# Two rounds of 32 tokens for expert pairs of 33 to 64, and a router that chooses tile by tile, in a float32 kernel of four layers

## What is computed

```
g_prob = softmax(t @ rg_w + rg_b)                     # 4 groups
g_p, g_idx = top_k(g_prob, 1)
e_logits = (t @ re_w + re_b).reshape(n_tok, 4, 8)[chosen group]
e_p, e_idx = top_k(softmax(e_logits), 2)              # 2 of the group's 8 experts
gate = g_p * e_p / sum(e_p);   expert = g_idx * 8 + e_idx
# each expert e, on the tokens that chose it:
hg, hu = split(x @ w_gu[e], 2)                        # 1024 -> 512 and 512
y = (silu(hg) * hu) @ w_down[e]                       # 512 -> 1024
out = sum over a token's two experts of gate * y
```

## Time and profile before

| | us |
|---|---|
| median of 3 runs | 2333.54 |
| lowest, highest | 2332.27, 2340.67 |
| the profiled execution | 2336.21 |
| its span, first to last instruction | 2334.4 |

### The profile page before, as it was taken

One profiled execution on the slowest core, in us unless ns is written; L12 is line 12 of the kernel. 1 busy time (PEld: TensorE's weight loads), 2 busy tenths in 40 slices (PEclk: granted clock), 3 DMA queues, 4 the chain that ended last, 5 costly groups with the idle time before them and its releaser, 6 DMA issues.

```text
span 2334.4 us, 30929 instructions
## 1 busy us (share of the span) xinstructions
PE 1858.1 (80%) x13622; PEld 1234.3 (53%) x13622; DVE 594.2 (25%) x964; ACT 388.7 (17%) x738; POOL 17.0 (1%) x18
## 2 busy tenths in 40 slices
PE   7999999999999875766666887599986575876664
PEld 5788875788876644222224563475983233622211
DVE  1223222224221343121111101455345221111112
ACT  2233102233111221100000000142221000000001
POOL 0000000000000000000000000001000000000000
PEclk9999999999999966888878998799997798989887
DMA  8312343422344306999999674213013799699996
GB/s 320 104 73 102 146 162 133 114 77 106 133 177 185 122 0 244 427 424 426 424 426 421 242 289 185 73 45 136 5 60 136 326 424 425 240 387 424 425 425 251
DMA packets 51160, 539.59 MB, mean 231 GB/s; under 512 B 7393, under 2 KB 16097, under 8 KB 17665
## 3 DMA queue, kind: packets, MB, share of 16 engines
q1 hardware_dynamic: 49248, 527.13, 55.8%
q0 software_dynamic: 864, 6.29, 0.7%
q10 hardware_dynamic: 832, 2.98, 0.3%
HBM read 535.33 MB, written 1.05 MB: 230 GB/s over the span
## 4 chain that ended last, share of the span: by engine, by line
PE 68%; DMA 16%; DVE 6%; issue 6%; ACT 4%; DVEq 0%; ACTq 0%
PE ps L399 50%; PE ps L406 16%; DMA arena<-in_moe_w_down 4%; DMA arena<-in_moe_w_gu 4%; DMA ring<-in_moe_w_gu 4%; DMA ring<-in_moe_w_down 3%; PE ps L412 2%; DVE arena L1254 2%; DVE x L1265 1%; ACT arena L2003 1%; ACT arena L2007 1%; DVE mT L1254 1%; ACT hb L2003 1%; ACT L2003 0%; DVE hb L1254 0%
## 5 line engine op out<-in xcount | busy, mean ns | idle before, releaser
L399 PE MATMUL ps<-hT,ring 128*128 128x256 f32 (+2 forms) x1888 | 389.5, 371 | 0.0
L399 PEld LDWEIGHTS ps<-hT,ring 128*128 128x128 f32 (+2 forms) x1888 | 329.2, 184 | 53.2 <-issue 3.4
L406 PE MATMUL ps<-arena 128*32 128x512 f32 (+2 forms) x1556 | 255.9, 706 | 121.2 <-issue 86.3
L406 PE MATMUL ps<-ring,arena 128*32 128x512 f32 (+1 forms) x1440 | 219.9, 683 | 99.2 <-issue 69.9
L2007 ACT ACTIVATE arena<-ps 128x512 f32<-128x512 f32 (+3 forms) x139 | 90.9, 654 | 905.0 <-PE ps L406 540.0
L1254 DVE TENSOR_TENSOR arena<-arena,ps 128x256 f32<-128x256 f32 (+3 forms) x88 | 51.7, 588 | 704.1 <-ACT arena L2003 610.0
L406 PEld LDWEIGHTS ps<-arena 128*32 128x32 f32 (+2 forms) x1556 | 68.6, 132 | 286.3 <-issue 232.0
L399 PE MATMUL ps<-arena 64*64 64x64 f32 (+10 forms) x1808 | 169.5, 299 | 51.2 <-ACT arena L2266 22.3
L406 PEld LDWEIGHTS ps<-ring,arena 128*32 128x32 f32 (+1 forms) x1440 | 62.2, 126 | 238.4 <-issue 197.3
L399 PEld LDWEIGHTS ps<-arena 64*64 64x64 f32 (+3 forms) x1808 | 114.0, 167 | 107.8 <-ACT arena L2266 50.6
L399 PE MATMUL ps<-ring,hT 128*128 128x256 f32 (+4 forms) x576 | 151.4, 422 | 8.7 <-ACT hT L2003 7.0
(11 more groups left out here) (150 smaller groups left out, 1397.8 us busy)
## 6 DMA issues: line engine op xcount, KB each, us to landing
ring<-in_moe_w_gu SPq DMA_DIRECT2D x64, 2048.0 KB, 26.3
arena<-in_moe_w_gu SPq DMA_DIRECT2D x64, 2048.0 KB, 29.0
arena<-in_moe_w_down SPq DMA_DIRECT2D x32, 2048.0 KB, 31.0
ring<-in_moe_w_down SPq DMA_DIRECT2D x32, 2048.0 KB, 30.4
ring<-in_w_merge SPq DMA_DIRECT2D x16, 2048.0 KB, 7.7
ring<-in_w_in SPq DMA_DIRECT2D x10, 2048.0 KB, 7.4
ring<-in_attn_w_qkv SPq DMA_DIRECT2D x6, 2048.0 KB, 8.0
ring<-in_rw_w_rkv SPq DMA_DIRECT2D x6, 2048.0 KB, 7.3
```

Source lines behind the costliest of these rows:

```text
L399: i = t.matmul(o, l, r, start=first, stop=last, skip_group_check=True)
L406: i = t.matmul(o, l, r, start=first, stop=last, skip_group_check=True)
```

## The change

Four edits:

1. **Middle path.** It now serves pairs of 33 to 64 tokens (`2 * CAP`, CAP is 32), in two rounds on each weight chunk. Round 0 takes the 32 tokens that are already in `xe`; only tokens 32 to 63 are gathered (into `x2`). All its matmuls have the small path's form, once for each round.
2. **Full path.** Its text is the same, but it serves pairs of more than 64 tokens, where it served those of more than 128.
3. **Router.** Each tile's router matmuls stand right behind its transposes in `out_proj`, and VectorE chooses tile by tile, with 16 operations for each. A rising table (1000 - index) lets one scalar_tensor_tensor and a maximum find the first of the greatest.
4. **Behind the first gather.** Both Exp calls, the gate values and the flags come after the one-hot matrix on which the gather waits (`"0 oh"`). The names `"da end"` and `"rw end"` now stand ahead of the layer norms, and the waits of all engines for each other at the start of `moe` are gone.

The core of the diff:

```
-            p = tile(name, (act, name + " out a"), (dve, name + " out b"))
...
+            p = tile(f"moe{l} route{i}", (dve, f"moe{l} logits{i}"))
+            t.wait_ge(*act(name + " out a"))
+            t.wait_ge(*dve(name + " out b"))
+            mm([(p[:, 0:36], hT[:, k, i * P:(i + 1) * P], m.rw36[:, l, k, :], k == 0, k == KT - 1) for k in range(KT)], f"moe{l} route{i}")
...
-        t.wait_ge(*dve(M + "0 places"))
+        t.wait_ge(*dve(M + "0 oh"))
         for half in range(2):
             gather(psum[0][:, 512 * half:512 * half + 512], half, M + f"first gather{half}")
+        t.wait_ge(*dve(M + "0 places"))
         gates_T(psum[1][:, 0:512], M + "first gatesT")
...
-                    lst = [(buf[:, k * P:(k + 1) * P], x[:, i, k * P:(k + 1) * P], oh24[:, i, a, :], i == 0, i == 1)
-                           for a, buf in enumerate((pg, pt)) for k in range(KT) for i in range(NT)]
+                    lst = [(psum[1][:, k * 64:(k + 1) * 64], x[:, i, k * P:(k + 1) * P], e.oh2[:, i * 64:(i + 1) * 64], i == 0, i == 1)
+                           for k in range(KT) for i in range(NT)]
...
-                        mm_to([(bufs[a][:, n * P:(n + 1) * P], gv[q][:, kk, a * D + n * P:a * D + (n + 1) * P], e.xm[a][:, 2 * q + kk, :],
-                                q + kk == 0 and n % 4 == 0, q == 3 and kk == 1) for kk in range(2) for a in range(2) for n in range(8)],
-                              before + 8 + q, N + f"gu{q}")
+                        mm_to([(pg[64 * a + 32 * c:64 * a + 32 * c + 32, 512 * r:512 * r + 512], xs[r][:, 2 * q + kk, a, :],
+                                gv[q][:, kk, a * D + c * 512:a * D + (c + 1) * 512], q + kk == 0, q == 3 and kk == 1)
+                               for kk in range(2) for r in range(2) for a in range(2) for c in range(2)], before + 8 + q, N + f"gu{q}")
+                    t.wait_ge(*act(N + "m gu"))
+                    tr([(psum[0][:, (4 * r + k) * P:(4 * r + k + 1) * P], g[:, k * P:(k + 1) * P], idn)
+                        for r, g in enumerate((e.gu, e.gu2)) for k in range(4)], N + "m guT")
...
+                        mm_to([(psum[1][64 * n + 32 * a:64 * n + 32 * a + 32, 512 * r:512 * r + 512], hs[r][:, 2 * q + kk, a, :],
+                                dv[q][:, kk, a * D + n * 512:a * D + (n + 1) * 512], q + kk == 0, q + kk == 2)
+                               for kk in range(2) for r in range(2) for n in range(2) for a in range(2)], before + 20 + q, N + f"dn{q}")
...
+        def first_of(dst, val, rising, top):
+            stt(eq, val, top, rising, ALU.is_ge, MUL)
+            red(ix, eq, MAX)
+            ts(dst, eq, ix, None, ALU.is_equal, None)
...
+            ts(cnt2, cnt, 2 * CAP + 0.5, None, ALU.is_gt, None)
```

More of the change, by code:

```diff
@@ L167, in take, with last @@
         return self.tiles[i], old
+    def last(self, name):
+        self.of[name] = len(self.tiles) - 1
+        return self.tiles[-1]
     def __call__(self, name):
@@ L815, in part @@
             return go
-        out_proj("da", d.oT, [(i, part(i)) for i in (1, 0)])
+        out_proj("da", 0, d.oT, [(i, part(i)) for i in (1, 0)])
     def moe(l):
         e, M = m.moe, f"moe{l} "
-        p = tile(M + "route", (dve, M + "logits"))
-        mm(proj_tok(hT, m.rw36[:, l], KT, [p[:, i * 512:i * 512 + 36] for i in range(NT)], slice(0, 36)), M + "route")
         sel = e.sel
-        p = tile(M + "count", (dve, M + "count"))
-        t.wait_ge(*dve(M + "gates"))
+        p = ps.last(M + "count")
+        for i in range(NT):
+            t.wait_ge(*dve(M + f"sel{i}"))
         mm([(p[:, 0:32], tab["st1"], sel[:, 0, :], True, True),
@@ L1210, in part @@
             return go
-        out_proj("rw", r.kT, [(i, part(i)) for i in range(NT)])
+        out_proj("rw", 1, r.kT, [(i, part(i)) for i in range(NT)])
     t.wait_ge(m.consts_landed, 32)
@@ L1561, in layer_norm, with out_proj @@
             stt(x[:, i, :], x[:, i, :], ss[i][:, 1:2], m.lnr[:, 1, :], MUL, ADD, name(i))
-    def out_proj(n, rows, parts):
+    def out_proj(n, l, rows, parts):
         for _, part in parts:
             part()
+        dve.name(f"{n} end")
         for i, _ in parts:
@@ L1570, in out_proj @@
             cp(m.hT[:, 4:8, i * P:(i + 1) * P], ps(f"{n} xT{i}")[:, 512:1024].rearrange("p (k s) -> p k s", k=4), f"{n} xT{i} out b")
-        dve.name(f"{n} end")
-        v.wait_ge(*pe(f"{n} end"))
-        v.wait_ge(*act(f"{n} end"))
+        for i, _ in parts:
+            route(l, i)
     def oT_out(n, dst, i):
@@ L1782, in moe @@
                     after_own()
-                    v.tensor_tensor(acc[:, 1, :], acc[:, 1, :], pt, ADD).then_inc(*dve.to(before + 20, N1 + "all in"))
+                    v.tensor_tensor(acc[:, 1, :], acc[:, 1, :], pg, ADD).then_inc(*dve.to(before + 20, N1 + "all in"))
             with v.Else():
@@ L1972, in part @@
             return go
-        out_proj("rw", 4, [(i, part(i)) for i in range(NT)])
+        out_proj("rw", 1, 4, [(i, part(i)) for i in range(NT)])
     v.wait_ge(m.consts_landed, 32)
@@ L2181, in out_proj @@
             part()
+        act.name(f"{n} end")
         for i, _ in parts:
@@ L2245, in moe @@
         psum = ps.tiles
-        act.name(M + "start")
         g4 = e.ex[:, :, 0:4]
-        s.wait_ge(*dve(M + "group in"))
-        fn(g4, g4, ACT.Exp, M + "group exp")
-        s.wait_ge(*dve(M + "second in"))
-        fn(e.m2, e.m2, ACT.Exp, M + "second exp")
-        act.name(M + "routed")
-        s.wait_ge(*pe(M + "routed"))
-        s.wait_ge(*dve(M + "routed"))
+        s.wait_ge(*dve(M + "gates in"))
+        fn(g4, g4, ACT.Exp)
+        fn(e.m2, e.m2, ACT.Exp, M + "gates exp")
         pg, pt = psum[2], psum[3]
```

191 lines of the change are left out of this document (86 added, 105 removed).

## The result

| | before | changed |
|---|---|---|
| median, us | 2336.4 (4 runs) | 2301.7 (4 runs, 2300.5 to 2302.6) |
| ratio, 95% interval | | 0.9851 [0.9829, 0.9873] |
| profiled execution, us | 2336.2 | 2301.5 |
| its span | 2334.4 | 2299.6 |

The change makes the kernel 34.7 us faster (1.5%); 59.8 were forecast. 2301.7 lies 3.7 us above the range. The two spans differ by 34.8 us, which is to be split by place.

What follows compares the result with a forecast made beforehand. The weight stream was taken as the bound, except at both routers, three middle pairs and the first MoE's end. Routers -26.0, first MoE's pairs -3.8 and pair 5 -30.0 summed to -59.8, forecast 2275 us, range 2260 to 2298.

Steps and rivals of the forecast that it cites:

- -13.0: Each MoE's router, from last hT copy to first gather: 13.0 us less, passed on to the weight stream.
- a gain of 13.2 ... Both routers: -26.0: Router stretch falls from 23.5 to 10.3 us, taken as 13.0 for each of two routers, all reaching the end.
- It fits by 1.3 us: At the first router, six weight chunks land near 914.3, 1.3 us before the first used slot comes free at 915.6.
- +25.5: First MoE's pair 12, now on the full path: 25.5 us slower, bounds +21 to +33.
- the tail 6.9: Behind pair 12's full path, the stretch from its down matmuls to pair 13 takes 6.9 us.
- What is late next is nothing: Behind pair 12, gu slots come free late, at 1329, but loads still arrive before pair 13 wants them.
- -29.3: First MoE's pair 14, now in two rounds: 47.3 us for 76.6, bounds 43 and 60.
- rivals 2 and 3: Two rounds: weight loads lie bare (2322 us, chance 0.02), or rounds run one after another (2400, slower, chance 0.02).
- I take -30: Second MoE's pair 5, now in two rounds: 30 us gained at the end, bounds -24 to -30.6.
- The loss of 30.6 goes to about 0: The weight stream's loss of 30.6 us in the second MoE's pair 5 nearly vanishes, as slots come free sooner.
- Rival 1: Half the routers' gain, pair 12 at +33, pair 5 at -24: 2303 us; chance 0.16 together with rival 5.
- rival 5: Second MoE gains nothing from pair 5, as the stream loses time elsewhere: 2306 us; chance 0.16 together with Rival 1.

Runs made afterwards that it cites:

- e4: The changed kernel without flags and branch at pair 0 of each MoE, which takes the small path; ratio 0.9831 to the kernel before.
- e15: The changed kernel with each MoE's seventh and later weight loads held until TensorE has used pair 0's first gu chunk; ratio 0.9923 to the kernel before.
- e5: The changed kernel with the first MoE's pair 14 weight loads held until TensorE has used pair 13's first gu chunk; ratio 0.9844 to the kernel before.
- e10: e5 with the two inner paths in the other code order, two rounds first and full path behind them; one execution of 2299.3 us.

## Why the prediction was wrong

The gains came where they were forecast, and four terms were too good; what two of them left out is the wait for the code behind a branch. Their errors, 8.4 + 11.0 + 4.2 + 5.5 = 29.1 us, less 4.2 of small gains that no step had, are the 24.9 between -59.8 and -34.9.

1. **"-13.0" for each router: 8.3 (8.7 by pair 11) and 8.9.** The failed step is "a gain of 13.2 ... Both routers: -26.0", which counts up to the gather and lets all that follows move with it. The choice took 7.7 us for 7.0, the gather began 12.6 earlier. But before, the first eight loads were over ahead of the gather, and the packet with the branch's code landed beside it (923.8). Now the gather runs while they still come in. The packet lands with their end, and the first `gu` began 3 us behind it in seven places: 2.4 us back. Without the branch the gap is gone (e4), and with the loads over earlier it shrinks by 2.4 and 2.2 us (e15). The prediction had looked at these loads ("It fits by 1.3 us") as data for TensorE, not as a queue ahead of its code. The first 16 `gu` records then ran at a granted clock of 0.65 for 1.00: 1.9 us back. The second MoE gave back 2.7 and 0.8.
2. **"+25.5" for pair 12: +36.5, above the bound of +33.** The failed step is "the tail 6.9": 15.84. 6.1 of the 8.9 more are two weight loads at the same moment (e5), the other 3 the code that the full path's way out jumps over (e10: 9.76 to 6.84). The upper bound allowed 4 us around the waits, drawn from gaps behind another path. Start and `gu` were right to 0.4 us, `dn` 1.5 longer. "What is late next is nothing" was right of the data and wrong of the code.
3. **"-29.3" for pair 14: -25.1.** The mechanism held: 128 records without bare weight loads or serial rounds, so rivals 2 and 3 are out. The sizes: gather and copies 9.1 for 7.2, `gu` 16.0 for 14.1, `dn` 8.8 for 7.3, the gap between 5.2 for 6.3. The excess is in the first records behind a pause: 8 of them take 1.71 us, later 0.86, with a granted clock of 0.50 to 0.59 in these stretches (1.2 of 2.4 GHz). I had taken the rates of the small path's fast rows.
4. **"I take -30" for pair 5: -24.5**, at its bound of -24. The failed step is "The loss of 30.6 goes to about 0", and that all of it reaches the end. 2.8 us of the loss stayed, in the slice behind the gap of 9.70, during which the slots filled. In that gap the two packets land 5.2 and 5.9 us behind the last matmul, where before they landed 2.4 and 3.8 behind; why was not tested. So the stream gained 27.3. Then 2.9 came back behind the last chunk, 1.6 in slow records and 1.3 in the write of the output, to which the prediction gave nothing.

Rival 1 was the nearest: it named gaps behind a branch and the full path's upper end, and gave 2303. It had a share of 0.16 together with rival 5. That its number came within 2 us is in part luck. It gave the routers 4.6 us too little and pairs 12 and 14 together 7.7 too much, and with 4.2 of small gains that it did not have these nearly cancel. The reserve of 1.3 us that it thought thin held for the data: the weights were in at 911.5, and TensorE used the first chunk only at 914.28.

## What to carry to other kernels

A taken branch has a price in the profile (mostly 5 to 7 us of "issue" here) that other work hides or bares; when a change moves it, ask what work hid it before, which loads are issued beside it, and which blocks of code lie between. Cost a stage up to the event on which the bound resource waits, not up to the moved operation. A path that was fast only when the clock was up should be costed from rows that follow a pause like its own.

## What the runs showed of the hardware

- Code arrives by DMA in packets of 16 KB (4 for 0.07 MB on the queue "instruction"). That the packets of q8 are TensorE's is inferred from the times: in eleven rows above its first instruction behind a branch follows one by 2.4 to 3.0 us. Weight loads issued at the jump delay them: a gap behind a jump of 9.76 us without loads is 15.84 with two of 2.1 MB. Loads that have long been under way need not: at 20 ends of pairs in the full stream the gap is 4.7 to 5.4 us. The Trainium skill (Runtime: NRT & Kernel Launch, Instruction fetch mechanics) says that a taken branch whose target is not in the current window of two pages forces a DMA fetch before execution goes on, and that the blocks are of 16 KiB; the packets agree.
- The order of code blocks moves these gaps from path to path: putting the full path last took 2.9 us from behind it and 2.9 from ahead of the two rounds' gather, and added 4.4 behind the two rounds, in one execution. A third packet goes with each longer gap.
